# Four norms of a transformer kernel: the last output tile, its statistics and the first new x in two token halves

## The reference

```python
x = x + rms_norm(m, g[1])            # m: the output of a mixer or an MLP
h = rms_norm(x, g[2])                # enters the next stage's matmul
def rms_norm(x, g):
    y = x * lax.rsqrt(jnp.mean(x * x, axis=-1, keepdims=True) + EPS)
    return y * g
```

## Time and profile before

| | us |
|---|---|
| median of 3 runs | 1744.0 (1743.93 to 1744.01) |
| the profiled execution, its time | 1742.19 |
| its span, first to last instruction | 1740.4 |
| TensorE busy | 1716.7 (99%) |
| VectorE, ScalarE, GpSimd busy | 1076.9, 775.7, 949.1 |
| mean granted TensorE clock | 0.995 of full |

### The profile page before, as it was taken

One profiled execution on the slowest core, in us unless ns is written; L12 is line 12 of the kernel. 1 busy time (PEld: TensorE's weight loads), 2 busy tenths in 40 slices (PEclk: granted clock), 3 DMA queues, 4 the chain that ended last, 5 costly groups with the idle time before them and its releaser, 6 DMA issues.

```text
span 1740.4 us, 25887 instructions
## 1 busy us (share of the span) xinstructions
PE 1716.7 (99%) x9327; PEld 1481.2 (85%) x9327; DVE 1076.9 (62%) x1693; ACT 775.7 (45%) x1301; POOL 949.1 (55%) x583
## 2 busy tenths in 40 slices
PE   8999999999999999999999999999999999999999
PEld 6887888989898887778898989989888888888887
DVE  6458657766667779956867676767765254444100
ACT  6338645343434666554544344455366332222221
POOL 3457546555556679755655545575445554444442
PEclk9999999999999999999999999999999999999999
DMA  5522121423232222212231323222210232222332
GB/s 186 137 101 62 34 76 61 146 68 127 74 133 71 99 73 85 97 64 83 85 134 61 134 83 111 85 85 73 100 37 27 83 109 96 96 96 96 105 101 72
DMA packets 46103, 158.84 MB, mean 91 GB/s; under 512 B 5744, under 2 KB 6000, under 8 KB 46000
## 3 DMA queue, kind: packets, MB, share of 16 engines
q1 hardware_dynamic: 46000, 157.45, 27.0%
HBM read 153.10 MB, written 2.10 MB: 89 GB/s over the span
## 4 chain that ended last, share of the span: by engine, by line
PE 84%; DVE 6%; POOL 4%; ACT 2%; issue 2%; DMA 0%; SPq 0%; POOLq 0%; DVEq 0%; ACTq 0%
PE PS L2199 24%; PE PS L2200 24%; PE PS L2201 24%; DVE PS L1461 2%; PE PS L2268 2%; PE PS L2304 1%; POOL acc_p L790 1%; PE PS L2299 1%; PE PS L2300 1%; PE PS L2209 1%; POOL wl L778 1%; PE PS L2461 1%; POOL acc_p L818 1%; DVE PS L1453 1%; PE PS L2241 0%
## 5 line engine op out<-in xcount | busy, mean ns | idle before, releaser
L2200 PE MATMUL PS<-XLR,wh 128*128 128x512 f32 x1216 | 473.3, 389 | 0.0
L638 POOL TENSOR_TENSOR wl<-raw,wh 128x1024 fp32r<-128x1024 f32 x96 | 232.9, 2428 | 261.4 <-ACT wh L1432 120.8
L628 POOL TENSOR_TENSOR wl<-raw,wh 128x1024 fp32r<-128x1024 f32 x105 | 252.9, 2415 | 184.2 <-ACT wh L890 184.1
L2199 PE MATMUL PS<-XHR,wh 128*128 128x512 f32 x888 | 347.5, 391 | 1.4 <-POOL wl L778 1.0
L2201 PE MATMUL PS<-XHR,wl 128*128 128x512 f32 x888 | 345.7, 389 | 0.0
L890 ACT ACTIVATE wh<-raw 128x1024 fp32r<-128x1024 f32 x171 | 179.2, 1057 | 289.6 <-PE PS L2201 246.4
L2200 PEld LDWEIGHTS PS<-XLR,wh 128*128 128x128 f32 x1216 | 228.4, 188 | 46.7
L2199 PE MATMUL PS<-TH,wh 128*128 128x256 f32 (+1 forms) x872 | 250.5, 287 | 0.1
L2200 PE MATMUL PS<-TL,wh 128*128 128x256 f32 (+1 forms) x872 | 250.2, 287 | 0.0
L2201 PE MATMUL PS<-TH,wl 128*128 128x256 f32 (+1 forms) x872 | 250.2, 287 | 0.0
L2199 PEld LDWEIGHTS PS<-XHR,wh 128*128 128x128 f32 x888 | 166.7, 188 | 36.5 <-POOL wl L778 1.4
(11 more groups left out here) (373 smaller groups left out, 3402.2 us busy)
## 6 DMA issues: line engine op xcount, KB each, us to landing
raw<-weights SPq DMA_DIRECT2D x287, 512.0 KB, 3.3
X<-x_t SPq DMA_DIRECT2D x8, 256.0 KB, 6.8
out_t<-X SPq DMA_DIRECT2D x8, 256.0 KB, 4.3
KH<-rope_h SPq DMA_DIRECT2D x4, 128.0 KB, 4.8
KL<-rope_l SPq DMA_DIRECT2D x4, 128.0 KB, 5.5
QH<-XHR SPq DMA_DIRECT2D x16, 32.0 KB, 2.0
QL<-XLR SPq DMA_DIRECT2D x16, 32.0 KB, 2.0
pos_i<-positions SPq DMA_DIRECT2D x1, 256.0 KB, 8.6
```

Source lines behind the costliest of these rows:

```text
L628: pool.tensor_tensor(wl[:, WPOS[n]], raw[:, n % RING], wh[:, WPOS[n]].bitcast(F32), ALU.subtract).then_inc(w_lo, 1)
L638: pool.tensor_tensor(wl[:, s], raw[:, j], wh[:, s].bitcast(F32), ALU.subtract).then_inc(w_lo, 1)
L2199: pe.matmul(out, wa, xa, start=start, stop=False)
L2200: pe.matmul(out, wa, xb, start=False, stop=False)
```

## The change

At each of the four boundaries the last output tile is made in two halves of 256 tokens: LEFT into bank RB, RIGHT into a ring bank (`right_bank`, the one of the tile before the next stage's first). Each half has its own square, copy to M, statistics, root, reciprocal, spread and new x of tile k = 0. The left half's statistics stand in the middle of the right half's matmuls. At m2 and m4 (`DIRECT`) the last two of the seven squares are no longer added by GpSimd: TensorE reads sqb[:, 0] and sqb[:, 1] itself, and the last tile's squares go to tmp. The fillers go from 1 + 2 + 10 to 1 + 3. Two `hi` calls move: the one of the next stage's third block goes ahead of the last two squares at m2 and m4, that of its fourth behind the left half's copies at all four. On VectorE `last_output` copies and factors LEFT, then copies RIGHT. `last_down_tile` (m2, m4) is built as `last_tile` (m1, m3), with its two identity matmuls in each half and `stat_left` at k = 5. The diff, cut to the core:

```diff
+DIRECT = {"m2": 2, "m4": 2}
-W_SQUARE, W_FACTOR, W_UPDATE = 1, 2, 10
+W_SQUARE, W_UPDATE = 1, 3
 # TensorE
+            def last_tile(n, job):
+                open_block(n)
+                for half in (LEFT, RIGHT):
+                    if half is RIGHT:
+                        open_tile(TILE0[AFTER_NORM[job]] - 1)
+                    for k in range(KT):
+                        if half is RIGHT and k == 4:
+                            stat_left(job)
+                        ins = products(PS[:, RB if half is LEFT else right_bank(job), half], *weight(n, k), XH[:, k, half], XL[:, k, half], k == 0, k == KT - 1)
+                    if half is LEFT:
+                        ins.then_inc(left_made, 1)
+                ins.then_inc(blocks_done, 1)
+            def stat_part(job, columns):
+                parts_of = [ssq[:]] + ([sqb[:, 0], sqb[:, 1]] if job in DIRECT else []) + [last_squares(job)]
+                for i, x in enumerate(parts_of):
+                    for j in columns:
+                        ins = pe.matmul(PS[:, STAT, j:j + 1], x[:, j * P:(j + 1) * P], ones[:, 0:1],
+                                        start=(i, j) == (0, columns[0]), stop=(i, j) == (len(parts_of) - 1, columns[-1]))
             def norm_out(job, next_phase, opened=False):
-                pe.wait_ge(ssq_adds, SSQ_ADDS[n])
-                pe.wait_ge(sd_done, n)
-                for j in range(4):
-                    pe.matmul(PS[:, STAT, j:j + 1], ssq[:, j * P:(j + 1) * P], ones[:, 0:1], start=j == 0, stop=False)
+                pe.wait_ge(left_rcol, b + 1)
+                pe.wait_ge(left_kept, b + 1)
+                spread_part(job, (0, 1)).then_inc(left_rb, 1)
                 keep_busy(W_SQUARE, PS[:, T % 4])
-                pe.wait_ge(last_sq, OUTPUTS.index(job) + 1)
-                for j in range(4):
-                    ins = pe.matmul(PS[:, STAT, j:j + 1], sqb[:, 0, j * P:(j + 1) * P], ones[:, 0:1],
-                                    start=False, stop=j == 3)
-                ins.then_inc(stat_done, 1)
-                keep_busy(W_FACTOR, PS[:, T % 4])
-                pe.wait_ge(bank_free, T)
-                spread(job)
+                pe.wait_ge(left_sd, b + 1)
+                pe.wait_ge(last_sq, b + 1)
+                stat_part(job, (2, 3)).then_inc(stat_done, 1)
                 keep_busy(W_UPDATE, PS[:, T % 4])
             def enter_residual(phase, entry):
+                pe.wait_ge(left_xh, R2N[entry])
+                for half in (LEFT, RIGHT):
+                    if half is RIGHT:
+                        pe.wait_ge(xh, x0 + 1)
+                    for t in range(3):
...
+                        pe.matmul(PS[:, (T0 + t) % 4, half], wh[:, WPOS[n0 + t], 0], XH[:, 0, half],
+                                  start=half is LEFT, stop=False)
+                    if half is LEFT:
+                        spread_right(job)
+                    for t in range(2):
+                        pe.matmul(PS[:, (T0 + t) % 4, half], wl[:, WPOS[n0 + t], 0], XH[:, 0, half], start=False, stop=False)
+                pe.matmul(PS[:, (T0 + 2) % 4], wl[:, WPOS[n0 + 2], 0], XH[:, 0], start=False, stop=False)
+                for k in range(1, KT + 1):
...
 # ScalarE
+            def early_operand(entry, block):
+                sc.wait_ge(left_new, b + 1)
+                sc.activation(XH[:, 0, LEFT], new_x(0)[:, LEFT], ACT.Copy, scale=ENTRY_GAIN[entry](0)).then_inc(left_xh, 1)
+                sc.activation(X[:, 0, LEFT], new_x(0)[:, LEFT], ACT.Copy).then_inc(left_x_kept, 1)
+                hi(block)
+                sc.wait_ge(x_new, kept)
+                sc.activation(XH[:, 0, RIGHT], new_right(entry), ACT.Copy, scale=ENTRY_GAIN[entry](0)).then_inc(xh, 1)
+                sc.activation(X[:, 0, RIGHT], new_right(entry), ACT.Copy).then_inc(x_kept, 1)
...
+                sc.activation(ssq[:], X[:, 0], ACT.Square).then_inc(squares, 1)
-            def last_square(done, **kw):
+            def last_square(job, done, **kw):
+                sc.wait_ge(left_made, OUTPUTS.index(job) + 1)
+                sc.activation(last_squares(job)[:, LEFT], PS[:, RB, LEFT], ACT.Square, **kw).then_inc(left_sq, 1)
+                root_left(job)
                 sc.wait_ge(blocks_done, done)
-                sc.activation(sqb[:, 0], PS[:, RB], ACT.Square, **kw).then_inc(last_sq, 1)
+                sc.activation(last_squares(job)[:, RIGHT], PS[:, right_bank(job), RIGHT], ACT.Square, **kw).then_inc(last_sq, 1)
             def boundary(entry, n):
-                root("m" + entry[1])
-                hi(n + 3)
-                operand(entry)
+                root_right("m" + entry[1])
+                operand(entry, n + 3)
 # VectorE
+                    v.wait_ge(left_rb, r)
+                    update_half(LEFT, new_x(0)[:, LEFT], left_new)
+                    factor_right(job)
+                    v.wait_ge(rb_done, JOB[job] + 1)
+                    update_half(RIGHT, new_right(entry), x_new)
+                    for k in range(1, KT + 1):
+                        if k < KT:
+                            update(k)
+                        if k == 1:
+                            v.wait_ge(left_x_kept, r)
+                            split_half(LEFT, new_x(0)[:, LEFT])
+                            v.wait_ge(x_kept, KT * (r - 1) + 1)
+                            split_half(RIGHT, new_right(entry)).then_inc(xl, 1)
+                        else:
+                            split(k - 1)
 # GpSimd, at m2 and m4
-                add_output(job, KT - 3)
-                add_output(job, KT - 2)
+                pool.wait_ge(restored, KT // 2 * (layer + 1))
 # ScalarE, end of the MLP
                 hi(n + 2)
+                hi(n + 3)
                 square_m(5)
                 square_m(6)
-                sc.wait_ge(ssq_adds, SSQ_ADDS[JOB[job]] - 1)
-                last_square(n + 1)
-                hi(n + 3)
+                last_square(job, n + 1)
```

More of the change, by code:

```diff
@@ L922, in keep_r2, with operand @@
                 sc.activation(r2[:], PS[:, RB], form).then_inc(r2_done, 1)
-            def operand(entry):
-                for k in range(KT):
+            def operand(entry, block=None):
+                if entry in M_GAIN:
+                    early_operand(entry, block)
+                for k in range(1 if entry in M_GAIN else 0, KT):
                     if entry == "x5":
@@ L1306, in _ @@
             sc.activation(exp_first[:], vec[:, 0:1], ACT.Sqrt)
[L1307 removed]
+            last_square("m3", BLOCK0["pw2"] + 8, bias=col("b_pw2", KT - 1))
             mlp(1, "x3", "m4")
@@ L1723, in last_output, with take @@
                 n = OUTPUTS.index(job) + 1
-                v.wait_ge(last_sq, n)
[L1725 to L1730, removed]
+                def take(half, bank):
+                    if bias:
+                        return ts(M[:, KT - 1, half], PS[:, bank, half], bias(KT - 1), ALU.add)
+                    return v.tensor_copy(M[:, KT - 1, half], PS[:, bank, half])
+                v.wait_ge(left_sq, n)
+                take(LEFT, RB).then_inc(left_kept, 1)
+                factor_left(job)
+                v.wait_ge(last_sq, n)
+                take(RIGHT, right_bank(job)).then_inc(bank_free, 1 + skip)
+                v.wait_ge(left_kept, n)
+                v.wait_ge(bank_free, T + 1)
             def outputs(phase, job, bias=None):
@@ L2516, in _ @@
             y_ready = {4 + t: (lambda t=t: pe.wait_ge(yl_done, t + 1)) for t in range(4)}
-            for m in range(KT):
-                tile(n0 + m, T0 + m, {} if m else y_ready, bank=PS[:, RB] if m == KT - 1 else None)
+            for m in range(KT - 1):
+                tile(n0 + m, T0 + m, {} if m else y_ready)
+            last_tile(n0 + KT - 1, "m1")
             norm_out("m1", "mlp0_up0")
@@ L2589, in down_tile, with last_down_tile @@
                         i = H21 if k % 2 else H11
-                        ins = products(bank, *weight(n, k), parts(TH, p, i, 2), parts(TL, p, i, 2),
-                                       k == 0 and not kept, k == SLOTS - 1)
+                        ins = products(bank, *weight(n, k), parts(TH, p, i, 2), parts(TL, p, i, 2), k == 0, k == SLOTS - 1)
                     ins.then_inc(blocks_done, 1 + SKIP.get(n, 0))
+                def last_down_tile(n):
+                    open_block(n)
+                    pe.wait_ge(last_m_lo, layer + 1)
+                    for h, half in enumerate((LEFT, RIGHT)):
+                        if h:
+                            pe.wait_ge(products_read, READS * (QUAD0[down_block(layer, NCHUNK - 1)[0]] + QUADS - 1))
+                        bank = PS[:, right_bank(out_job) if h else RB, half]
+                        pe.matmul(bank, ident_r[:], parts(TH, LAST_M, H11 + h), start=True, stop=False)
+                        pe.matmul(bank, ident_r[:], parts(TL, LAST_M, H11 + h), start=False, stop=False)
+                        for k in range(SLOTS):
+                            if h and k == 5:
```

(11 more changed lines are left out.)

110 lines of the change are left out of this document (80 added, 30 removed).

## The result

The changed kernel takes 1750.6 us (median of 7 runs, 1748.88 to 1752.61) against 1743.95 for the kernel before (7 runs, 1742.45 to 1746.12): ratio 1.0036 [1.0025, 1.0047], 6.6 us slower. A second set gave 1752.4 (5 runs) against 1744.9 (15 runs), 1.0045 [1.0032, 1.0059]. Forecast were 1747.9 and a range of 1743.0 to 1752.0: the sign and the mechanism of parts 1 to 4 held, and 2.7 us were missing from the sum. For that mechanism by itself the prediction had given 1746.4 to 1749.5; 1750.6 lies above it, on the way to the 1751.3 of rival R1 (more falls of the clock). The profiled execution after took 1751.02 (span 1749.0) at a mean granted clock of 0.991, that of before 1742.19 at 0.995.

A forecast was written before the change was run, and what follows sets the result against it. TensorE was taken to bound the kernel, with VectorE pacing it at each boundary's entry up to k = 3; 0.68 + 0.96 + 0.82 + 0.9 + 0.5 = 3.9 us on 1744.0 gave 1747.9, range 1743.0 to 1752.0.

The forecast's parts named there:

- rival R1: More clock falls over products of k = 1 to 3: 1.7 us each, 1751.3 with two; chance 0.17.
- Part 1: Last tile in halves: 256-column products at 0.12 us, +0.32 at first and third boundary, +0.35 at second and fourth.
- Part 2: Left statistics inside the tile at full length: 0.90 us at first and third boundary, 1.80 at second and fourth.
- Rival R3: Left statistics hide among the tile's short products: 1742 to 1744, or partly, 1745 to 1747; chance 0.20.
- Part 3: From tile's end to VectorE's right update: later by 1.33 us at the first boundary, 1.79 at the second.
- branch (a): First boundary, behind the right square: TensorE's right statistics 245.60, root 246.6, right reciprocal 247.2.
- (b): First boundary: VectorE's right copy and left update, ScalarE's left copy, three left products, right spread at 247.98; 0.7 behind branch (a).
- part 6: Granted clock falls to 0.50 at the second boundary, over left products and right spread: 0.5 us; none at the fourth.
- Part 4: TensorE late from k = 3 on, after give-back and slack: 0.68, 0.96, 0.82, 0.9 us at the four boundaries.
- Part 5: Removed GpSimd adds and fillers, and moved `hi` calls, around the boundaries: counted at nothing.
- Rival R2: TensorE paces the entry, so its 1.7 us earlier first product is kept at all four boundaries: 1737; chance 0.08.
- the prediction's last sign of being wrong: At the boundaries' entry: the prediction is wrong if TensorE runs at half clock after k = 1.

The follow-up runs named there:

- e4: The kernel before with its last tile's products in two token halves and nothing else: 1747.8 us, ratio 1.0017.
- e1: The changed kernel with the right spread ahead of the three left products on TensorE: 1747.2 us, ratio 1.0010.
- e3: The changed kernel with ten more 256-column fillers, seven ahead of the right products and three ahead of k = 1: 1746.6 us, ratio 1.0014.
- e7: e6 with e3's ten fillers added: 1745.0 us, ratio 1.0000.
- e9: e8 with e3's ten fillers added: 1744.2 us, ratio 0.9996.
- e5: The kernel before with three fillers after the spread in place of ten: 1745.8 us, ratio 1.0009.
- e6: e1 with the right statistics of all sources but the last ahead of the wait for the right square: 1742.75 us, ratio 0.9992.
- e8: e6 with VectorE's right copy to M moved behind the left update: 1745.8 us, ratio 1.0012.
- e2: The changed kernel with the last two squares left out of the sums at m2 and m4 (incomplete computation): 1745.8 us, ratio 1.0006.

## Why the prediction was right, and where its size was off

Times in before's time: less 2.38 at the first boundary, less 3.31 at the second.

**Part 1, the tile in halves: right.** 0.33 and 0.29 measured in e4, 0.32 said. The row decided against the figure of the Trainium skill (TensorE: Matmul & The Clock Gate, "Back-to-back issue gap"), which the page gives for a matmul by itself and by which, as an estimate, the tile would have been 0.2 shorter; e4 agrees with the row.

**Part 2, the left statistics at full length: right.** The tile's last product starts at 247.15 - 2.38 = 244.77 (said 244.80) and at 594.07 - 3.31 = 590.76 (said 590.82). Rival R3 falls with it.

**Part 3, the right factor: right at the first boundary.** VectorE's right update starts at 248.49 (said 248.40), behind a spread that stands behind three left products. e1 took that step out and got 0.79 back, at 247.70: near the 247.6 that branch (a) gives with the reciprocal done at 247.2 and 0.4 for the spread. (The prediction puts (b) 0.7 behind (a); its own times, 247.98 and 247.2, make 0.8.) At the second it is 598.93 - 3.31 = 595.62, 0.58 behind the 595.04. Up to the left products it came as said (597.54 - 3.31 = 594.23, said 594.26); from 597.4 the clock stands at 0.50, so the 0.5 of part 6 is this one.

**Part 4, what TensorE loses: 0.94 and 1.04 for 0.68 and 0.82.** This is a term too small by 0.2. k = 3 starts at 258.46 - 2.38 = 256.08 against 255.28: 0.80 late, 0.12 more than said, most of it VectorE's 0.09. The other part is on TensorE. Where the first product had to wait for its operand the second starts 0.33 after it (253.99 and 254.32, 258.46 and 258.80), not 0.23; before had such waits at k = 0 and 1 alone, and after has them to k = 3. At 258.46 the product's wait is too short to be marked, but that of its weight load is not:

```profile
258.46 0.19 PEld L2411 LDWEIGHTS PS<-XHR,wh 128*128 128x128 f32 x1 [0.27 <-ACT XHR L979]
```

Its six products take 259.95 - 258.46 = 1.49; before's take 1.38, from 255.28 to this row:

```profile
256.66 0.84 PE L2304 MATMUL PS<-XLR,wh 128*128 128x512 f32 x3
```

That 0.11 was to be had from the trace of before, whose products of k = 0 show it:

```profile
249.34 0.50 PE L2299 MATMUL PS<-XHR,wh 128*128 128x512 f32 x1
249.67 0.40 PE L2300 MATMUL PS<-XHR,wl 128*128 128x512 f32 x1
```

With the full clock (e3) the four cost 4.1 where parts 1 to 4 said 3.4. The 2.38 that the trace was late by ahead of the first boundary is not the change's. Busy time of the first 25 us, before and then after:

```profile
0.00:25.00 25.00, 18.93 (x70) 14.20 (x71) 16.94 (x23) 15.88 (x23) 1.71 (x13) 1.00 0.75 273
```

```profile
0.00:25.00 25.00, 19.04 (x60) 13.85 (x61) 16.29 (x22) 15.87 (x23) 1.70 (x13) 0.86 0.77 273
```

By 10 us after is 0.75 late, behind an x transfer that landed later (ScalarE waits for it until 9.22, in before until 8.46); the rest came while its products stood 0.43 apart, until 16.7. e3, e7 and e9, with the same code up to the first boundary, start at -0.13, -0.06 and -0.16. A 1.00 in such a row is no proof of the full clock: the profile has no granted clock ahead of its first record (18.8 us in e1), and prints 1.00 there. The row of e1 for the same 25 us has 1.00 too, yet its products stood 0.43 apart until 18.4, and it is 3.39 late:

```profile
17.99 0.63 PE L2480 MATMUL PS<-XHR,wh 128*128 128x512 f32 x1
18.42 0.57 PE L2481 MATMUL PS<-XLR,wh 128*128 128x512 f32 x1
```

**Part 5, what goes at nothing: right.** ScalarE's timeline of after has the two squares of the MLP's end and the left square in a row, behind VectorE's restore and not behind the moved weight copies:

```profile
585.36 2.14 ACT L908 ACTIVATE wh<-raw 128x1024 fp32r<-128x1024 f32 x2
589.09 1.15 ACT L1240 ACTIVATE sqb<-M 128x512 f32<-128x512 f32 x2 [1.58 <-DVE M L1499]
590.14 0.37 ACT L1176 ACTIVATE tmp<-PS 128x256 f32<-128x256 f32 x1
```

The fillers that went cost nothing at the full clock (e5). Whether all 1 + 2 + 10 of them, left in the changed kernel, would have kept its clock was not run; e3's are others, in other places.

**Part 6, the clock: the step that was mis-sized.** Said were 0.5 at the second boundary and 0 at the fourth, because "the fourth lies otherwise in time". Measured: 6.8 us at 0.50 at both, in both traces of the changed kernel, 1.2 and 1.3 each against e3, 2.5 in all. The place was wrong as well: I let the fall end with the left products, and it runs on through k = 1, where each product takes 0.42 for 0.23. It ends there: k = 2 has its products 0.23 apart again (605.21 and 605.44), so the prediction's last sign of being wrong, half clock after k = 1, did not come. This is rival R1, at a smaller price than its 1.7 for a fall. The measured time lies inside the range because R1's two falls had been given room in it, not because part 6 forecast them. Three comparisons agree on the price: e6's second boundary against e7's (1.51 and 0.29), e8's first against e9's (1.03 and -0.18), and the changed kernel against e3: 1.2 to 1.3 each.

The sum in place of 3.9 is 4.1 + 2.5 = 6.6, counted like the forecast from the one trace of before.

**Rival R2** needed the right update at 247.70 to break even. e1 put it exactly there, at 247.70, and its first boundary cost 0.12: the point was placed to about 0.1, and the changed kernel is 0.8 on the wrong side of it.

**Open.** How much of e4's 3.9 is the clock in its other runs, and whether any is the halves'; why the fillers give 4 to 5 us when the boundaries show 2.5; and what decides at which of the boundaries the clock falls in an execution: the six traces in the changed order without the added fillers (changed twice, e1, e2, e6, e8) show 2, 2, 0, 1, 1 and 1 falls at the four boundaries, the three with them (e3, e7, e9) none. That fillers prevent the falls is likely by this, with one trace each.

## What to carry to other kernels

Before splitting the last step of a chain to start its consumer earlier, find who paces the consumer once it runs, and follow when *that* engine gets all it needs: here TensorE could start 1.8 us earlier and lost 0.9, because VectorE got the second half's factor later than it once got the whole. Look in each engine's written order for a short instruction (a spread) that stands behind a wait of another branch; moving one line took 2.5 of the structure's 4.1 us away (e1's 1.6 against e3's 4.1, both at the full clock, one trace each). Whoever shortens or thins the work around a wait should cost the granted clock at every such place, with its price read where products, not waits, run at the low level.

## What the hardware showed

- A product of 512 columns starts 0.23 us after its neighbour in a stream, but where the first one waited for its operand the second starts only 0.33 us after it, in both kernels (before 249.34 and 249.67; after 258.46 and 258.80).
- At 0.50 (1.2 GHz) products of 512 columns stand 0.42 apart, at 1.00 (2.4 GHz) 0.23. A stretch of 3.4 or 6.8 us at 0.50 in an entry cost 1.2 to 1.3 us; some of it falls into waits (the 0.51 ahead of k = 1 at the first boundary are gone at the second). Amid products 6.8 us at 0.50 cost 2.5 (e6, from 146.6 on, in code that no edit touches: of its "start" of 2.78 only 0.25 were there before).
- Where the clock falls changes between executions of one kernel. The kernel before took 1741.3 to 1748.8 in 35 runs, at mean clocks of 0.993 to 0.996, and a profiled execution was up to 3.4 us late ahead of any change ("start" in the table).
